# A decoder step on one core: column 21 of the feed-forward as a ninth pair, and earlier splits of down weights beside plain columns

## The reference

```python
def conv_ffn(h, prefix, w_up, conv_w, conv_b, w_down):
    up = h @ w_up
    c, new_state = causal_dwconv(up, prefix, conv_w, conv_b)
    g, u = c[..., :D_FF], c[..., D_FF:]
    return (jax.nn.silu(g) * u) @ w_down, new_state
```

## Time and profile before

| | |
|---|---|
| median of 3 runs | 877.42 us (877.25 to 877.79) |
| profiled execution | 876.97 us |
| its span, first to last instruction | 875.1 us |
| TensorE (matmuls) busy | 850.4 us, 97% |
| VectorE busy | 554.5 us, 63% |
| ScalarE busy | 363.6 us, 42% |
| mean granted clock of TensorE | 0.996 |

### The profile page before, as it was taken

The page is one execution under the profiler, slowest core; times in us unless marked ns, Lnnn a source line. Parts: engine busy times, 40 slices in busy tenths (PEclk is TensorE's granted clock), DMA queues, the critical chain, the costliest instruction groups (busy, mean ns, idle before and its releaser), DMA issues.

```text
span 875.1 us, 17354 instructions
## 1 busy us (share of the span) xinstructions
PE 850.4 (97%) x6884; PEld 799.7 (91%) x6884; DVE 554.5 (63%) x981; ACT 363.6 (42%) x652; POOL 68.8 (8%) x149
## 2 busy tenths in 40 slices
PE   7999999999999999999999999999999999999995
PEld 7988878789999999877999999999999999999994
DVE  6344246677584732465455998778678696786754
ACT  7302133465553611354343754335244343452452
POOL 2320000000000000000000320100001001010200
PEclk9999999999999999999999999999999999999998
DMA  8798698731234555598233322232223322332222
GB/s 306 262 364 292 218 323 315 240 98 49 55 98 136 166 206 187 169 359 315 65 94 124 98 61 73 85 121 73 85 73 109 98 79 79 108 88 63 88 73 103
DMA packets 50146, 131.25 MB, mean 150 GB/s; under 512 B 5939, under 2 KB 8503, under 8 KB 49810
## 3 DMA queue, kind: packets, MB, share of 16 engines
q1 hardware_dynamic: 48064, 124.40, 43.1%
q0 software_dynamic: 1712, 5.62, 1.8%
q10 hardware_dynamic: 290, 0.12, 0.1%
HBM read 123.12 MB, written 7.00 MB: 149 GB/s over the span
## 4 chain that ended last, share of the span: by engine, by line
PE 69%; DVE 9%; ACT 4%; issue 3%; DVEq 0%; ACTq 0%
PE proj L1177 41%; PE proj L1133 3%; PE proj L1194 2%; PE proj L1196 2%; PE proj L1195 2%; DVE w_lo L1864 2%; PE score L1428 2%; PE score L1261 1%; PE score L1259 1%; PE score L1260 1%; PE T L1261 1%; PE T L1260 1%; PE T L1259 1%; PE score L1394 1%; DVE conv L2027 1%
## 5 line engine op out<-in xcount | busy, mean ns | idle before, releaser
L1177 PE MATMUL proj<-a_hi,w_hi 128*128 128x272 f32 (+1 forms) x740 | 160.7, 292 | 12.6 <-DVE w_lo L1864 6.3
L1528 ACT ACTIVATE w_hi<-w_raw 128x1024 fp32r<-128x1024 f32 (+2 forms) x128 | 119.0, 931 | 109.2 <-PE proj L1177 79.7
L1864 DVE TENSOR_TENSOR w_lo<-w_raw,w_hi 128x1024 fp32r<-128x1024 f32 (+2 forms) x128 | 136.9, 1070 | 34.7 <-ACT w_hi L1528 34.5
L1177 PE MATMUL proj<-a_lo,w_hi 128*128 128x272 f32 (+1 forms) x740 | 158.2, 288 | 0.0
L1177 PE MATMUL proj<-a_hi,w_lo 128*128 128x272 f32 (+1 forms) x740 | 158.0, 288 | 0.0
L1177 PEld LDWEIGHTS proj<-a_hi,w_hi 128*128 128x128 f32 x740 | 118.5, 189 | 20.9 <-DVE w_lo L1864 8.0
L1177 PEld LDWEIGHTS proj<-a_lo,w_hi 128*128 128x128 f32 x740 | 118.8, 189 | 0.0
L1177 PEld LDWEIGHTS proj<-a_hi,w_lo 128*128 128x128 f32 x740 | 118.4, 189 | 0.0
L1177 PE MATMUL proj<-d_hi,w_hi 128*128 128x272 f32 x448 | 92.4, 287 | 0.0
L1177 PE MATMUL proj<-d_lo,w_hi 128*128 128x272 f32 x448 | 92.1, 287 | 0.0
L1177 PE MATMUL proj<-d_hi,w_lo 128*128 128x272 f32 x448 | 92.1, 288 | 0.0
(11 more groups left out here) (360 smaller groups left out, 1653.0 us busy)
## 6 DMA issues: line engine op xcount, KB each, us to landing
w_raw<-in_w_up SPq DMA_DIRECT2D x28, 512.0 KB, 3.6
w_raw<-in_w_in SPq DMA_DIRECT2D x21, 512.0 KB, 3.9
early_pages<-in_cache_k SPq DMA_DIRECT2D x32, 256.0 KB, 6.2
pages<-in_cache_v SPq DMA_DIRECT2D x32, 256.0 KB, 5.3
c_pages<-in_cache_mem_k SPq DMA_DIRECT2D x16, 512.0 KB, 6.7
c_pages<-in_cache_mem_v SPq DMA_DIRECT2D x16, 512.0 KB, 5.8
p_raw<-in_w_up SPq DMA_DIRECT2D x16, 512.0 KB, 3.9
w_raw<-in_w_down SPq DMA_DIRECT2D x32, 256.0 KB, 2.6
```

The source lines that it names most:

```text
L1177: mm = pe.matmul(tile_banks(n)[:, half, 0:width], wt, act[:, at, half * HALF:half * HALF + width], start=(k == 0 and a == 0), stop=(k == w ...
L1528: act.activation(w_hi[:, n % W_HI_RING, 0:kt, :], w_raw[:, n % W_RING, 0:kt, :], ACT.Copy).then_inc(w_hi_ready, 1)
L1864: dve.tensor_tensor(w_lo[:, n % W_RING, 0:kt, :], w_raw[:, n % W_RING, 0:kt, :], w_hi[:, n % W_HI_RING, 0:kt, :].bitcast(F32), ALU.subtrac ...
```

## The change

Column 21 joins `PAIRED`, so it is done in seven products. `beside_of` deals the eight tiles of `down3` to columns 16 to 21 as 1, 2, 1, 2, 0, 2 (before: 2, 2, 2, 2, 0, 0). Beside a plain column that a pair follows and that has two down tiles (4, 6, 8, 10, 12, 14), both down tiles' splits now stand in the steps of the gate tile, and none in those of the up tile. Column 20's activation is split after the last tile of `down3`. The tiles are 130 now, since two up-projection tiles have become a pair.

```diff
--- before.py
+++ after.py
@@ -39,7 +39,7 @@
 GROUPS, GB = 2, 4
 SELF_UNITS = SEQ // P * HEADS
 FFN_GROUPS = [range(0, 4), range(4, 8), range(8, 12), range(12, 16), range(16, 22)]
-PAIRED = list(range(5, 20, 2))
+PAIRED = list(range(5, 22, 2))
 DIST = 384
 W_RING, W_HI_RING = 4, 3
 C_PAGE_RING = 8
@@ -84,14 +84,18 @@
 
 
 
+LAST_BESIDE = (1, 2, 1, 2, 0, 2)
 LAST_DOWN = f"down{len(FFN_GROUPS) - 1}"
 
 
 def beside_of(i):
 
     g = next(g for g, group in enumerate(FFN_GROUPS) if i in group)
-    j = i - FFN_GROUPS[g][0]
-    return [(f"down{g - 1}", "add", n) for n in (2 * j, 2 * j + 1)] if g and j < 4 else []
+    if g == 0:
+        return []
+    counts = LAST_BESIDE if g == len(FFN_GROUPS) - 1 else (2,) * 4
+    first = sum(counts[:i - FFN_GROUPS[g][0]])
+    return [(f"down{g - 1}", "add", n) for n in range(first, first + counts[i - FFN_GROUPS[g][0]])]
 
 
 def make_ffn_order():
@@ -375,6 +379,8 @@
             if q is not None and FFN_ORDER[j - 1][2] == 6:
                 late = f + 2
                 s += hi + [("add", f)]
+                if not beside_of(PAIRED[q] - 1) and PAIRED[q] > len(FFN_GROUPS[0]):
+                    s.append(("act", PAIRED[q] - 1))
             else:
                 s += hi + lo + [("add", f)]
                 if q is not None:
@@ -389,6 +395,9 @@
         soon = PAIRED.index(i + 1) if i + 1 in PAIRED else None
         if not second and i == 0:
             s.append(("norm", "up"))
+        if soon is not None and len(beside_of(i)) == 2:
+            after_hi, after_lo = split_next(f + 1)
+            hi, lo = ([], []) if second else (hi + after_hi, lo + after_lo)
         s += hi + [("up_in", i, int(second))] + lo
         if second and soon is not None:
             s.append(("pair_split", soon, 0))
@@ -404,7 +413,8 @@
             if not beside_of(i):
                 if soon is not None:
                     s.append(("pair_split", soon, 2))
-                s.append(("act", i))
+                if soon is None or not beside_of(i + 1):
+                    s.append(("act", i))
 
     s += [("half_tile", TILE[LAST_DOWN, "add", n]) for n in range(2)]
     for n in range(KT - 1):
```

## The result

The changed kernel takes 882.86 us (879.13 to 886.17, 14 runs), the kernel before, run beside it, 878.28 (877.17 to 880.61, 14 runs): 1.0053 times as long, interval 1.0036 to 1.0070. That is 4.6 us slower; forecast were 1.7, and the range ended at 881.0. The profiled execution is one of the short ones, 879.91 us with a span of 878.1, 3.0 more than before.

A forecast was written before the change was run, and what follows sets the result against it. TensorE, busy 97% of the span, was taken as the bound, so only fewer matmuls or waits save time. Terms -6.6 + 2.3 + 5.1 - 1.4 + 1.2 = +0.6, plus 1.1 for the clock, gave +1.7: 879.1 us, range 877.0 to 881.0.

The forecast's parts named there:

- Parts one to five: Sum without TensorE's clock: earlier splits, columns 16 and 18, column 20, column 21's arithmetic and its end; +0.6 us together.
- The six waits: TensorE's waits for the second down tile's `w_lo` in groups two to four would go with the earlier splits: -6.6 us.
- Columns 16 and 18: With one down tile each, the pair's first product waits 1.94 us for `p_lo`; 2.06 replaces 0.92, twice: +2.3 us.
- Column 20: No down tile before the pair's first product, so it starts 4.95 us late waiting for `p_lo`; with the restart +5.1 us.
- Last activation: End of column 21: as a pair it gives both outputs late, a wait of 1.1 us and the restart: +1.2 us.
- Seven products: Column 21's arithmetic: seven products of 12 matmuls (10.6 us) replace two column tiles of 48 (11.95 us): -1.4 us.
- Part six: TensorE's clock falls in column 20's long wait; 2.0 us of the low stretch lie in the silence, the rest costs +1.1.
- The low clock that lasts: Rival: after column 20's wait the clock stays low as long as at the start, sum +2.8, 880.2 us; chance 0.14.
- That the clock holds: Rival: the clock does not fall through column 20's silence, sum +0.6, 878.0 us; chance 0.24.
- the fast case: Rival: VectorE not late beside columns 16, 18 and 20; only 2.7 us wait beside 20, -5.8, 871.6 us; chance 0.09.
- `t_lo`: Rival: this next split is late too beside columns 16 and 18, product 5 waits, +3.7, 881.1 us; chance 0.08.

The follow-up runs named there:

- the kernel whose silences are filled: The changed kernel with extra matmuls (14, 14, 38 and 8) in its four new waits; 878.82 us beside 878.04, ratio 1.0010.
- a version without them: The changed kernel with VectorE's steps in the last group reordered (first splits earlier, both `up_in` ahead of the taps at the end); 869.40 us beside 878.02, ratio 0.9895.

## Why the prediction was wrong

**Parts one to five held.** The six waits gave 6.3, not 6.6: from column 4's first down tile to column 16's first tile TensorE takes 195.60 (528.96 to 724.56), before 201.89 (528.74 to 730.63). The first of them gave less, as the second down tile beside column 4 still started 0.23 late (532.20 instead of 531.97). Columns 16 and 18: product 1 due at 739.53, started at 741.47, 1.94 late, as worked out. Column 20: 5.35 late instead of 4.95, as VectorE lost another 0.46 before the gate of column 19. Last activation: 1.18 instead of 1.1. Seven products took what was counted. Together -6.3 + 2.3 + 5.5 - 1.4 + 1.3 = +1.4 in the profiled execution, with 1.5 for the clock 2.9 of the 3.0, and +0.8 in the median of the kernel whose silences are filled, where +0.6 was forecast.

**Part six failed**, in two steps. The first is the sentence that no wait of up to 1.5 us cost a fall, from which I passed over the waits of 1.9 that my own sum put beside columns 16 and 18, and looked only at the one of 4.9. The profiles show that 1.8 us of silence brings a fall in some places and none in others, five times in twelve. The second is the size. I let 2 us of the low clock lie in the silence; in the profiled run the clock fell only as work resumed, so the whole stretch was in use: products 1 and 2 took 4.64 us (809.01 to 813.65) instead of 3.02, 0.12 of it the restart, so 1.5 instead of 1.1. Every low stretch amid the work took 3.4 us or twice that in the profiles, so the 4.5 us read off the start was too long. (There the level was read from the pace alone: the clock column has 1.00 at the start, and two pairs of matmuls took 0.62 us where the others took 0.45 to 0.51, so not all of that loss need be the clock.) Nor need the silence take any part of the low time. It can: in the kernel without the earlier splits the clock fell 3.2 us before work resumed, and 3.7 us of work at the low clock were left of 6.8. So the term was not 1.1 but 1.5 times a number that differs from run to run: the profiled run had one (granted clock 0.994 over the span, before 0.996). The median of the 14 clocks is 0.991, so some 0.005 x 2 x 883 = 8.8 us more at half clock; at 0.2270 us a matmul for 0.1254 that is worth 4.0 us. It is an estimate, good to about 1 us, since 0.001 of the clock is worth 0.8. The filled kernel gives the same without it: 3.8 us between its +0.8 and the measured +4.6. The five slowest runs all have 0.989, the three fastest 0.994.

**The rivals.** The low clock that lasts (+2.8) came nearest in the sum and had 0.14, but 2.2 for a single fall was too much, where one cost 1.5; it reached neither the number of places nor the time. That the clock holds failed with the first long wait. VectorE was late as worked out, so the fast case fell, and `t_lo` came in time beside columns 16 and 18. The rule of the Trainium skill that was weighed ("TensorE: Matmul & The Clock Gate", section "HAM oscillation", where waits of 3 to 5 us bring the clock down) pointed the right way, yet the runs here go further: 1.8 us sufficed at times.

What stays open: which of two equal waits brings a fall, and why one silence of 3.4 us brought one low stretch and another two. None of the runs here tells that apart. The waits of 1.0 us brought no fall in any profile, but no kernel was made with them alone.

## What to carry to other kernels

When a change moves work that covers a wait on a busy TensorE, price the wait twice: its length, and the slow stretch that may follow, which here came even behind 1.8 us. One profile shows one draw of the clock; look at the granted clock of all runs before a few microseconds are explained by it. And before a down tile is taken from beside a step, write down when the slowest supplier's split ends and when it would be due: here this gave each new wait to a few tenths, and later a version without them.

## What the runs showed of the hardware that I had not expected

In these kernels silence on TensorE cost more than useless work: 74 extra matmuls in four waits made the changed kernel 4.0 us faster (882.86 to 878.82), and 28 in two waits of 1.8 us another one probably 2.1 (876.42 to 874.32). Between a kernel's first matmuls and its last, the low stretches seen in the profiles were all about 3.4 us long (eight of them) or twice that (two, one behind a silence of 3.4 us and one behind 5.1); two other silences of 3.4 us and one of 5.2 brought a single one. They began anywhere from 3.2 us before work resumed to 1.0 us after.
